# Hybrid trunk layer on one core: first tiles taken whole, attention's low halves on VectorE, pooled tiles ahead of squares, gate tiles in quarters, a place of its own for one last weight half

## The reference

```python
h = x @ w_in[i]
pool_out = multiscale_pool(h[..., COL_POOL:COL_Z], pool_w[i], pool_scale[i])
ssd_out = ssd_mixer(h[..., COL_Z:COL_XBC], h[..., COL_XBC:COL_DT], h[..., COL_DT:COL_Q], ...)
q, k, v = (h[..., COL_Q:COL_K], h[..., COL_K:COL_V], h[..., COL_V:IN_COLS])   # by heads of 64
sb_out = stick_breaking_attention(q, k, v).reshape(b_, s_, SB_WIDTH)
mix = jnp.concatenate([pool_out, ssd_out, sb_out], axis=-1) @ w_out[i]
x = layer_norm(DEEPNORM_ALPHA * x + mix, ln1_g[i], ln1_b[i])
ffn = conv_glu_ffn(x, ffn_w_up[i], ffn_conv_w[i], ffn_conv_b[i], ffn_w_down[i])
ple = jax.nn.sigmoid(x @ ple_w_gate[i]) * (p[i] @ ple_w_proj[i])
x = layer_norm(DEEPNORM_ALPHA * x + ffn + ple, ln2_g[i], ln2_b[i])
# conv_glu_ffn: up = causal_conv3(x @ w_up); (silu(gate half) * value half) @ w_down
# ssd_mixer: causal conv of 4 taps, SiLU, chunked state-space scan, times SiLU(z), RMS norm over two groups
# attention weights: exp(log_sigmoid(z) + sum of later log_sigmoid(-z)), strictly causal
```

## Time and profile before

| | us |
|---|---|
| median of 3 runs | 1339.45 |
| lowest, highest | 1339.34, 1344.62 |
| the profiled execution | 1344.1 |
| its span, first to last instruction | 1342.3 |
| PE busy | 1299.1 |
| DVE busy | 841.8 |
| ACT busy | 508.1 |
| POOL busy | 227.7 |

### The profile page before, as it was taken

One profiled execution on the slowest core, in us unless ns is written; L12 is line 12 of the kernel. 1 busy time (PEld: TensorE's weight loads), 2 busy tenths in 40 slices (PEclk: granted clock), 3 DMA queues, 4 the chain that ended last, 5 costly groups with the idle time before them and its releaser, 6 DMA issues.

```text
span 1342.3 us, 16727 instructions
## 1 busy us (share of the span) xinstructions
PE 1299.1 (97%) x6288; PEld 1027.5 (77%) x6288; DVE 841.8 (63%) x996; ACT 508.1 (38%) x778; POOL 227.7 (17%) x152
## 2 busy tenths in 40 slices
PE   6999999999989998999999999999999999999986
PEld 5776766777776887888888787878787787888886
DVE  4546645646388556423477777768676867677765
ACT  4435535547654225112333332424242333233421
POOL 0000000052310002500112111111112121211126
PEclk9999999999999998999999999999999999999998
DMA  5101000010003212111020111111120101011202
GB/s 232 47 32 32 32 32 32 32 48 16 1 16 111 79 49 95 60 32 47 16 79 32 63 40 55 47 47 63 47 77 33 63 31 63 31 63 47 94 32 95
DMA packets 22661, 71.97 MB, mean 54 GB/s; under 512 B 2512, under 2 KB 2768, under 8 KB 22608
## 3 DMA queue, kind: packets, MB, share of 16 engines
q1 hardware_dynamic: 22608, 71.22, 15.7%
HBM read 67.02 MB, written 4.19 MB: 53 GB/s over the span
## 4 chain that ended last, share of the span: by engine, by line
PE 72%; DVE 9%; ACT 3%; issue 2%; DMA 2%; DVEq 0%; SPq 0%; ACTq 0%
PE ps L696 13%; PE ps L698 13%; PE ps L697 13%; PE ps L1054 7%; PE ps L1055 7%; PE ps L1053 7%; PE ps L774 2%; PE ps L791 2%; DMA down_raw<-u_down 2%; DVE conv_ff L1864 1%; DVE w_lo L579 1%; PE ps L835 1%; PE ps L750 1%; ACT conv_ff L1454 1%; PE ps L1084 1%
## 5 line engine op out<-in xcount | busy, mean ns | idle before, releaser
L696 PE MATMUL ps<-x_hi,w_hi 128*128 128x512 f32 x336 | 140.1, 417 | 11.4 <-DVE x_lo L516 10.6
L698 PE MATMUL ps<-x_hi,w_lo 128*128 128x512 f32 x336 | 133.7, 398 | 0.0
L697 PE MATMUL ps<-x_lo,w_hi 128*128 128x512 f32 x336 | 133.5, 397 | 0.0
L1916 DVE TENSOR_TENSOR acc<-acc,ps 128x512 f32<-128x512 f32 x144 | 96.2, 685 | 53.0 <-PE ps L698 52.5
L1054 PE MATMUL ps<-mix_lo,w_hi 128*128 128x512 f32 x320 | 126.7, 396 | 0.0
L1053 PE MATMUL ps<-mix_hi,w_hi 128*128 128x512 f32 x320 | 126.7, 396 | 0.0
L1055 PE MATMUL ps<-mix_hi,w_lo 128*128 128x512 f32 x320 | 126.7, 396 | 0.0
L696 PE MATMUL ps<-h_hi,w_hi 128*128 128x512 f32 x288 | 114.8, 399 | 1.6 <-DVE acc L1916 1.6
L698 PE MATMUL ps<-h_hi,w_lo 128*128 128x512 f32 x288 | 114.1, 396 | 0.0
L697 PE MATMUL ps<-h_lo,w_hi 128*128 128x512 f32 x288 | 114.0, 396 | 0.0
L2191 POOL TENSOR_TENSOR weight_sums<-raw 128x512 f32<-128x512 f32 x20 | 29.1, 1456 | 494.2 <-DMA raw<-u_up 494.2
(11 more groups left out here) (263 smaller groups left out, 2841.5 us busy)
## 6 DMA issues: line engine op xcount, KB each, us to landing
raw<-u_up SPq DMA_DIRECT2D x44, 512.0 KB, 3.3
raw<-u_in SPq DMA_DIRECT2D x22, 512.0 KB, 3.3
down_raw<-u_down SPq DMA_DIRECT2D x40, 256.0 KB, 2.8
x_stage<-u_x SPq DMA_DIRECT2D x8, 512.0 KB, 7.8
raw<-u_out SPq DMA_DIRECT2D x8, 512.0 KB, 3.2
x_nat<-x_nat SPq DMA_DIRECT2D x8, 512.0 KB, 3.2
raw<-u_gate SPq DMA_DIRECT2D x8, 512.0 KB, 3.3
out<-o_norm SPq DMA_DIRECT2D x8, 512.0 KB, 2.6
```

The source lines that it names most:

```text
L696: mm(dst, w_hi, x_hi, start=first, stop=False)
L697: mm(dst, w_hi, x_lo, start=False, stop=False)
L698: return mm(dst, w_lo, x_hi, start=False, stop=last)
L1916: v.tensor_tensor(dst, dst, ps[:, DOWN_BANKS[k % 4], :], ALU.add).then_inc(dn_added, 1)
```

## The change

What it does:

1. The first weight tiles are q0, k0, v0. SP loads tile 0, x0, x1, tile 1, x2 and on. ACT and DVE split tile 0 and x0 in halves (`FIRST`), counted by `first_hi` and `first_lo`; PE takes tile 0 over x0, then x1, then tile 1 over both, then goes on as before. v0 is projected third, and its two transposes stand after the first scores.
2. Raw places are counted over weight units alone (`raw_place`, `raw_before`).
3. Attention's three low halves move from POOL to DVE: two after the first state pair, the third after the last state. `decayed(5)` goes ahead of `gated(0)`.
4. On ACT the pooled high halves alternate with the squares (square 0, pooled 0, square 1, pooled 1); on DVE `pool_low(0)` goes ahead of `gated(1)`, the two weight low halves behind it.
5. Gates 0 and 1 take their second 512 tokens in two quarters: both gates over row tiles 4 and 5 when six row tiles are split, then both over 6 and 7. Their projections write PSUM pairs 2 and 3 and don't wait for the sigmoids.
6. D0B and D1B of the tenth chunk get `down_raw_last`, loaded ahead of the last down tiles, once the product S2 of the last pair is done; then come the gain's broadcast, and the bias's once D1B is split.

The diff, cut to its core:

```diff
@@ -61,13 +61,14 @@
            ["p0", "p1", "dt", "C1", "z0", "z1", "z2"]]
-IN_TILES = ["v0", "q0", "k0"] + [t for w in WINDOWS for t in w]
+IN_TILES = ["q0", "k0", "v0"] + [t for w in WINDOWS for t in w]
 IN_COLS = {"q": COL_Q, "k": COL_K, "v": COL_V, "x": COL_XBC, "B": COL_XBC + SSD_W,
...
-UNITS = [("in", 0), ("in", 1)] + [("x", i) for i in range(KT)] + [("in", i) for i in range(2, len(IN_TILES))]
+UNITS = [("in", 0), ("x", 0), ("x", 1), ("in", 1)] + [("x", i) for i in range(2, KT)]
+UNITS += [("in", i) for i in range(2, len(IN_TILES))]
 OUT_ORDER = [5, 6, 7, 0, 1, 3, 2, 4]
@@ -122,9 +123,19 @@
+def proj_pair(j):
+    return 2 + j if j < 2 else ple_item("proj", j) % 2
 def raw_place(n):
-    return n if n < UNIT[("x", 0)] else n - KT
+    return sum(1 for u in UNITS[:n] if u[0] != "x")
+def raw_before(n):
+    return max(i for i in range(n) if UNITS[i][0] != "x" and raw_place(i) == raw_place(n) - RAWS)
@@ -135,7 +146,7 @@
     pro = []
-    for name in ("v0", "q0", "k0"):
+    for name in IN_TILES[:3]:
         for h in range(2):
@@ -380,6 +392,7 @@
     dn_raw = over("down_raw", [P, 2, HALF], 9)
+    dn_last = over("down_raw_last", [P, 2, HALF], 12)
     lng = over("ln2_gain", [P, D], 11)
@@ -516,8 +531,11 @@
+    FIRST = ((0, HALVES[0]), (0, HALVES[1]), (1, HALVES[0]), (1, HALVES[1]))
     raw_a, raw_b = (FFN0 + 4) % RAWS, (FFN0 + 5) % RAWS
-    loads_before = [sum(1 for n, u in enumerate(UNITS) if u[0] != "x" and n % RAWS == r) for r in range(RAWS)]
+    loads_before = [sum(1 for n, u in enumerate(UNITS) if u[0] != "x" and raw_place(n) % RAWS == r)
+                    for r in range(RAWS)]
@@ -528,6 +546,8 @@
+        if c == LASTC and not pp and o in (D0B, D1B):
+            return dn_last[:, (D0B, D1B).index(o), :]
         if c == LASTC and pp and o not in PRODUCTS:
@@ -540,6 +560,8 @@
             eng.wait_ge(raw_in[r], 16 * (loads_before[r] + 2 * LASTC + 1))
+        elif c == LASTC and o in (D0B, D1B):
+            eng.wait_ge(dn_last_in, 32)
         elif o in (A11, A12):
@@ -602,16 +624,18 @@
             if raw_place(n) >= RAWS:
-                eng.wait_ge(split_done, n - RAWS + 1 if raw_place(n) >= 2 * RAWS else n - KT - RAWS + 1)
-            eng.dma_start(raw[:, n % RAWS, :], unit_source(n)).then_inc(raw_in[n % RAWS], 16)
+                eng.wait_ge(split_done, raw_before(n) + 1)
+            r = raw_place(n) % RAWS
+            eng.dma_start(raw[:, r, :], unit_source(n)).then_inc(raw_in[r], 16)
...
         load_x(0)
-        load(1)
-        for i in range(1, KT):
+        load_x(1)
+        load(UNIT[("in", 1)])
+        for i in range(2, KT):
             load_x(i)
@@ -665,13 +689,14 @@
         load_up(LASTC, 1, 1)
+        eng.wait_ge(prod_full, product_count(LASTC, S2, 1))
+        for i in range(2):
+            eng.dma_start(dn_last[:, i, :], a["u_down"][2 * (LASTC - 1) + i][:, HALF:D]).then_inc(dn_last_in, 16)
         for i, (o, r) in enumerate(((S4, raw_a), (A22, raw_b))):
             eng.dma_start(raw[:, r, :], a["u_down"][2 * LASTC + i]).then_inc(raw_in[r], 16)
-        eng.wait_ge(op_lo_done, lo_count(LASTC, D1A, 0))
-        load_down(LASTC - 1, D0B)
-        eng.wait_ge(prod_full, product_count(LASTC, S2, 1))
         eng.dma_start(lng[:, :], a["ln2_g"].partition_broadcast(P)).then_inc(ln_in, 16)
+        eng.wait_ge(op_lo_done, lo_count(LASTC, D1B, 0))
         eng.dma_start(lnb[:, :], a["ln2_b"].partition_broadcast(P)).then_inc(ln_in, 16)
@@ -794,23 +819,40 @@
-        for kt in range(KT):
+        def rows(it, kt):
+            kind, name, h, p = it
+            c, s_, i = slice(kt * P, (kt + 1) * P), HALVES[h], IN_TILES.index(name)
+            last = three(bank_of(p), wh[:, i, c], wl[:, i, c], xh[:, kt, s_], xl[:, kt, s_], kt == 0, kt == KT - 1)
+            if kt == KT - 1:
+                last.then_inc(p_full, 1)
+        for h in range(2):
+            if h:
+                eng.wait_ge(split_done, 2)
+            else:
+                eng.wait_ge(first_lo, 3)
+            rows(PROLOGUE[h], 0)
+        eng.wait_ge(split_done, UNIT[("x", 1)] + 1)
+        for h in range(2):
+            rows(PROLOGUE[h], 1)
+        eng.wait_ge(split_done, UNIT[("in", 1)] + 1)
+        for kt in range(2):
+            for h in range(2):
+                rows(PROLOGUE[2 + h], kt)
+        for kt in range(2, KT):
             eng.wait_ge(split_done, UNIT[("x", kt)] + 1)
-            c = slice(kt * P, (kt + 1) * P)
-            for kind, name, h, p in PROLOGUE[:4]:
-                s_ = slice(h * HALF, (h + 1) * HALF)
-                i = IN_TILES.index(name)
-                last = three(bank_of(p), wh[:, i, c], wl[:, i, c], xh[:, kt, s_], xl[:, kt, s_],
-                             kt == 0, kt == KT - 1)
-                if kt == KT - 1:
-                    last.then_inc(p_full, 1)
-        for it in PROLOGUE[4:]:
-            if it[0] == "turn":
-                eng.wait_ge(const_in, 48)
+            for it in PROLOGUE[:4]:
+                rows(it, kt)
+        for it in PROLOGUE[4:6]:
             piece(it, 0, 1)
+        eng.wait_ge(const_in, 48)
         for t in range(NTICK + LAG):
                 z_scores(Z_AT[t])
+            if t == 0:
+                for it in PROLOGUE[6:]:
+                    piece(it, 0, 1)
             if t - 1 in TASK_AT:
@@ -974,27 +1016,26 @@
-        def column_tile(dst, slot, n, halves):
+        def column_tile(dst, slot, n, spans):
             eng.wait_ge(split_done, n + 1)
-            for h in halves:
-                s_ = slice(h * HALF, (h + 1) * HALF)
+            for s_ in spans:
                 for kt in range(KT):
...
-        def gate_item(j, halves=(0, 1)):
+        def gate_item(j, spans=HALVES):
             n = UNIT[("gate", j)]
-            last = column_tile(two(ple_item("gate", j) % 2), RING_OF[n] % RINGS, n, halves)
-            if 1 in halves:
+            last = column_tile(two(ple_item("gate", j) % 2), RING_OF[n] % RINGS, n, spans)
+            if spans[-1].stop == S:
                 last.then_inc(u_full, 1)
...
-            dst = two(ple_item("proj", j) % 2)
+            dst = two(proj_pair(j))
             c = slice(j * P, (j + 1) * P)
@@ -1004,22 +1045,19 @@
         eng.wait_ge(x1_split, MT // 2)
-        gate_item(0, (0,))
+        gate_item(0, HALVES[:1])
         back(MT - 1)
         eng.wait_ge(y_read, MT)
-        gate_item(1, (0,))
-        eng.wait_ge(x1_split, MT)
-        gate_item(0, (1,))
-        gate_item(1, (1,))
+        gate_item(1, HALVES[:1])
+        for q in (2, 3):
+            eng.wait_ge(x1_split, 2 * q + 2)
+            for j in range(2):
+                gate_item(j, (slice(q * QUARTER, (q + 1) * QUARTER),))
         eng.wait_ge(split_done, UNIT[("proj", 1)] + 1)
         for j in range(2):
-            eng.wait_ge(sig_done, j + 1)
             proj_item(j)
         for j in range(2, KT):
-            if j == 2:
-                eng.wait_ge(u_free, 1)
-            else:
-                eng.wait_ge(sig_done, j)
+            eng.wait_ge(sig_done, j - 1 if j == 2 else j)
             gate_item(j)
@@ -1223,7 +1261,14 @@
-        for n in range(UNIT[("in", 2)]):
+        for i, (n, s_) in enumerate(FIRST):
+            eng.wait_ge(x_raw[0] if n else raw_in[0], 16)
+            ins = act(unit_place(n, False)[:, s_], unit_raw(n)[:, s_], ACT.Copy)
+            if i < 3:
+                ins.then_inc(first_hi, 1)
+            else:
+                ins.then_inc(hi_done, 2)
+        for n in range(2, UNIT[("in", 2)]):
             hi(n)
@@ -1232,7 +1277,8 @@
         hi(UNIT[("in", 4)])
-        for it in PROLOGUE[4:]:
+        for it in PROLOGUE[4:6]:
+            wait_evacuated(eng, it[3] - 2)
             evacuate(it)
@@ -1276,6 +1322,9 @@
             if n in Z_AT:
+                if n == 0:
+                    for it in PROLOGUE[6:]:
+                        evacuate(it)
                 sticks(Z_AT[n], 0)
@@ -1382,11 +1431,14 @@
         hi(UNIT[("out", 6)])
-        squared(0)
-        squared(1)
-        for k in range(2):
+        def pooled_high(k):
             src, free = task("po%d" % k)
             act(mh[:, k, :], src, ACT.Copy, scale=param("pool_scale", k)).then_inc(mixh, 1)
+        squared(0)
+        pooled_high(0)
+        squared(1)
+        pooled_high(1)
         hi(UNIT[("out", 7)])
@@ -1626,7 +1678,18 @@
         link(v.memset(zero[:, :], 0.0))
-        for n in range(UNIT[("in", 2)] + 1):
+        for i, (n, s_) in enumerate(FIRST):
+            if i < 3:
+                eng.wait_ge(first_hi, i + 1)
+            else:
+                eng.wait_ge(hi_done, 2)
+            ins = v.tensor_tensor(unit_place(n, True)[:, s_], unit_raw(n)[:, s_], unit_place(n, False)[:, s_].bitcast(F32),
+                                  ALU.subtract)
+            if i < 3:
+                ins.then_inc(first_lo, 1)
+            else:
+                ins.then_inc(split_done, 2)
+        for n in range(2, UNIT[("in", 2)] + 1):
             lo(n)
@@ -1729,7 +1792,15 @@
+        def attended_low(k):
```

(22 more changed lines are left out.)

11 lines of the change are left out of this document (7 added, 4 removed).

## The result

| | before | changed |
|---|---|---|
| median on the same chip, us | 1341.77 (4 runs) | 1328.19 (4 runs) |
| lowest, highest | 1339.34, 1344.62 | 1326.2, 1330.03 |
| the profiled execution | 1344.1 | 1330.03 |
| its span | 1342.3 | 1328.0 |

The ratio of changed to before is 0.9897, with a 95% interval of 0.9874 to 0.9919: faster by about 1%. The forecast was 1320.4 and its range, 1316 to 1329, holds 1328.19 near its upper end.

What follows compares the result with a forecast made beforehand. The prediction took PE, 97% busy, as the bound, with gains only from its waits and lower-clock stretches. Terms 4.4 + 4.4 + 6.1 + 4.1 = 19.0 us off the median 1339.45 gave 1320.4 us, range 1316 to 1329.

Steps and rivals of the forecast that it cites:

- What bounds the kernel: Whole kernel: PE is 97% busy, so gains come only from its waits, about 35 us, and slow stretches behind them.
- Start: First tiles: PE starts at 7.0 instead of 10.56 and a transpose wait goes; 4.4 us, bounds 2.5 to 4.8.
- Rival 3: Start: small gaps between split waits lengthen the slow stretch; gain 0.9 us instead of 4.4, 1324.0; chance 0.06.
- rival 4: Start: PE stays at 1.2 GHz, kernel 0.5% slower, 1346 us and up; chance 0.02.
- Attention's low halves: State-space stage: off POOL, state multiplies return to 0.56 us; with the sixth decay's move 5.5 us so far.
- Rival 2: State-space stage: POOL did not cause the slow states; the part gives 0.6 us, 1324.3; chance 0.08.
- Pooled tiles ahead of squares: Norm matmuls: PE waits 2.6 us for a square instead; 4.4 of the stage's 5.5 us arrive.
- Gates: Gates' second halves in quarters: last split hidden, 3.67 us wait and slow stretch go; 6.1 us, bounds 5.0 to 6.3.
- rival 5: Gate items: gain given back as VectorE or POOL becomes the bound, 1 to 4 us at most, 1323; chance 0.06.
- Tail: Last chunk's down half in its own place: earlier tap, shorter wait ahead of last_h_lo; 4.1 us, bounds 1.1 to 4.5.
- rival 1: Tail: gain's broadcast delays the last weight half's load to 1271; 3.0 us less gain, 1323.5; chance 0.15.

Runs made afterwards that it cites:

- tail_undo: The changed kernel with the tail of before: D0B and D1B of the tenth chunk in down_raw, both broadcasts behind; 1326.49 us, ratio to before 0.9881.
- tail_order: The changed kernel with the last tiles' D1B taken behind the tap on ScalarE and VectorE, loads unchanged; 1326.74 us, ratio to before 0.989.
- att_pool: The changed kernel with attention's three low halves back on POOL; 1330.76 us, ratio to before 0.9926.
- squares: The changed kernel with the second gating ahead of the pooled low half, and the third gating and its square earlier; 1325.13 us, ratio to before 0.9864.
- gates_undo: The changed kernel with the second 512 tokens of gates 0 and 1 whole, behind the last split; 1333.3 us, ratio to before 0.9941.
- changed_again: The changed kernel run once more without any edit; 1326.17 us, ratio to before 0.9893.
- start_undo: The changed kernel with the start of before: v0 and q0 first, x0 split whole, transposes ahead of the first scores; 1333.44 us, ratio to before 0.9937.
- pooled_undo: The changed kernel with the older order of squares, pooled tiles and second gating on ScalarE and VectorE; 1330.63 us, ratio to before 0.9916.
- best: The changed kernel with earlier second gating and squares, gain's broadcast behind D1B's split, last tiles' D1B behind the tap; 1322.58 us, ratio to before 0.9856.

## Why the prediction was right or wrong

**What bounds the kernel: right.** Everything was won from single waits of PE and the slow stretches behind them. A wait of 3.65 us cost 5.3 us in one execution and 6.4 in another. The view's waits add up to 31.9 us, not 35. And "behind waits of 2.49 us and more that slow stretch is there" holds in the profile before, but not in general: behind 2.98 to 3.0 us at the norm's sums it is missing in three profiles (tail_undo, tail_order, att_pool).

**Start: right**, 4.17 to 4.22 us against 4.4. First matmul at 7.20 (forecast 7.0), issue wait gone, a 0.25 us wait in its place (0.2). The first matmul 0.2 us later than forecast is about the difference, with the 0.1 to 0.2 us at x1's low half. Rival 3 (nothing gained) didn't come, nor rival 4: at 11.31 us PE was at full speed, 4.1 us into its work, in the profile before 4.0 us into it.

**Attention's low halves: right, in mechanism and size.** The states fell to 0.56, the first moved low half waited for POOL's gate, cb's matmuls came at 372.00 (forecast: 376.2, less the start's 4.2, 372.0). Rival 2 is refuted by att_pool. That the sixth decay goes ahead of the first gating was not tried by itself; the 1.38 us wait of the earlier trace rows is gone in the trace.

**Pooled tiles ahead of squares: right in the sum, for the reason given.** The wait was 3.01 us for a square, where 2.6 had been forecast. The working already said that the reordering hands the wait from the pooled tile to the square, and that only 4.4 of 5.5 us would arrive; 4.24 did. That it came so close is in part luck: with the same code other executions give up to 5.4. What it didn't say is what squares shows: the 2.2 us of VectorE's idleness that it wrote down was avoidable, and 3.4 to 4.6 us more were to be had.

**Gates: right**, 6.36 against 6.1; in gates_undo, where the clock came back sooner behind the same wait, it is 5.3, still inside the part's bounds. No new wait in the gate items: rival 5 didn't come.

**Tail: wrong, by the whole term**: 4.1 forecast, -0.25 and -0.21 measured in the pair of profiles. The step that failed is "then ScalarE waits only for the load before it (landing 1268.0)". On before's clock that load landed at 1257.1 + 14.8 = 1271.9. The working had priced it, in rival 1, at 1271 with a chance of 0.15, and had given as a reason against it that two broadcasts had stood behind down_raw and only one behind this load. That reason didn't hold: with one load behind it, broadcast or plain, landings of 5.5 to 6.2 us occur in four of nine profiles; with none, in none of three. A second step was weak too: the 6.2 us in the earlier trace rows came from one execution. tail_undo has the same order of loads with about 4.0, changed_again the changed order with 4.0 as well. The rule that the working cited for this rival (the Trainium skill, DMA: Bandwidth & Descriptors, section Two DMAs through the same engine are not ordered: started in order, but pipelined) gives no time. The 4.0 to 6.2 us of one and the same load do not go against it, and do not test it. The rival should have had more than 0.15. In the changed kernel's more favourable profile (changed_again) the tail's gain against before's profile is 1.9 us from the MLP's first product to last_h (525.08 us against 1267.52 - 744.34 = 523.18) and 45.03 - 43.74 = 1.3 of slow stretch, 3.2 in all; in its other profile, none. Against an equally favourable execution of the tail before (tail_undo, 1.59 us of wait against 1.12), it is half a microsecond.

**The sum.** Between 1320.4 and 1328.19 lie 7.8 us: 2.3 because the median before is 1341.77 with the profiled execution among the runs and 1339.45 without it; 4.35 in the tail; 0.2 more behind it, in the slow stretch; 0.1 in the other three parts; 0.7 between span, run and median. The lower bounds of the four parts add up to 9.2 us and not to 10, which changes nothing here. The bias load, held behind D1B, was issued at 1260.28 and waited for by nobody, as forecast.

**What stays open.** Why the landing varies from execution to execution; why the clock falls behind a given wait in one execution and not in another, and in which stages it was down in the longer executions of start_undo and pooled_undo.

## What to carry to other kernels

When a wait for a transfer is removed, look at the next transfer in the same engine's queue and at what is issued right behind it: a large load that nobody needs soon, issued 0.4 us behind one that an engine is waiting for, is best moved behind that wait. It is one line, and the three profiles with it moved have no late landing. A landing time read off a single profile is one draw, and so is the slow stretch behind a wait; for a term that rests on either, take the same operation at other places or a second profile, and keep both values. When work is moved off a shared port, price the neighbour's slowed instructions and not only the moved ones: here three operations cost VectorE 5.0 us, 1.5 of them beside POOL's gate product, and gave it 3.65 back in the states. And where the working notes an idle stretch of the busiest helper engine (2.2 us ahead of the pooled low half), ask what could stand in it.

## What the runs showed of the hardware

**The slow stretch comes all at once, and not by the wait's length alone.** The last column of the landings' table covers the same matmuls in every kernel. Behind waits of up to 2.14 us it is 43.73 to 43.75 us (tail_undo with 1.59, tail_order and best with 1.19 too). Behind 2.57 us and more it is 45.03 (before, 3.02) to 46.48: 1.3 to 2.8 us more, in matmuls of 256 columns every 0.21 us in place of 0.118, which are the 1.2 and 2.4 GHz levels. The amount did not go by the wait's length: 46.48 stands behind 2.57 and behind 2.95, 45.24 behind 3.01. Nor did it come each time: behind 2.98 to 3.01 us at the norm's sums the clock stayed at 1.00 in three profiles (tail_undo, tail_order, att_pool), and behind 2.50 us ahead of the 16 matmuls in att_pool it was 0.79 over 8 us.

**A landing time is a spread, not a number.** The same 512 KB load, in the same place of the program, with the same load behind it, took 4.0, 4.1, 4.6, 5.0 (twice), 5.5, 5.9 and 6.2 us in eight profiles. With the load ahead of it landed as it was issued, and the next load 1.2 us behind it, it took 3.2 (tail_undo).
